# Results of the last two expert positions summed in idle PSUM banks by matmul; second layer's bias rows loaded as start values of its sums

## What is computed

```
sel_group = jnp.argmax(grp_score, axis=-1)                 # one of 4 groups
_, idx = lax.top_k(jnp.where(in_group, biased, -jnp.inf), TOP_K)   # two experts in it
wts = sel_aff / jnp.sum(sel_aff, axis=-1, keepdims=True)
for e in range(N_EXPERTS):
    he = jax.nn.silu(h @ w_gate[e]) * (h @ w_up[e])
    y = y + combine[..., e:e + 1] * (he @ w_down[e])
x_l = x_l + mod_l[5] * y_l
```

## Time and profile before

| | |
|---|---|
| median of 3 executions | 1031.48 us (1030.33 to 1037.86) |
| the profiled execution | 1036.62 us, its span 1034.8 us |
| mean granted TensorE clock | 0.853 of full speed |
| PE busy | 781.3 us (76%), 6820 instructions |
| DVE busy | 392.3 us (38%), 883 instructions |
| ACT busy | 178.6 us (17%) |
| POOL busy | 28.0 us (3%) |
| DMA | 320.53 MB, mean 310 GB/s |
| SP's queue | 282.88 MB, 69.9% of 16 engines' span |

### The profile page before, as it was taken

The page is one execution under the profiler, slowest core; times in us unless marked ns, Lnnn a source line. Parts: engine busy times, 40 slices in busy tenths (PEclk is TensorE's granted clock), DMA queues, the critical chain, the costliest instruction groups (busy, mean ns, idle before and its releaser), DMA issues.

```text
span 1034.8 us, 18303 instructions
## 1 busy us (share of the span) xinstructions
PE 781.3 (76%) x6820; PEld 433.2 (42%) x6821; DVE 392.3 (38%) x883; ACT 178.6 (17%) x381; POOL 28.0 (3%) x43
## 2 busy tenths in 40 slices
PE   3989899997959549976669953596478878798580
PEld 1534647544544225543235521272344444354240
DVE  2267879647978642120112101623512111121013
ACT  3211011115530201110111100420111111111001
POOL 0000000020000010000000001000000000000001
PEclk9899999799989669996779976799599898799785
DMA  9887988789507788589999899902789899999923
GB/s 346 297 300 254 343 296 286 274 303 320 213 1 269 302 342 346 215 350 415 418 417 414 337 416 396 404 20 102 294 307 365 325 416 417 414 417 415 415 82 127
DMA packets 102222, 320.53 MB, mean 310 GB/s; under 512 B 12315, under 2 KB 27547, under 8 KB 85667
## 3 DMA queue, kind: packets, MB, share of 16 engines
q1 hardware_dynamic: 78454, 282.88, 69.9%
q0 software_dynamic: 3952, 21.37, 5.4%
q10 hardware_dynamic: 19776, 15.75, 4.7%
HBM read 303.58 MB, written 24.64 MB: 317 GB/s over the span
## 4 chain that ended last, share of the span: by engine, by line
PE 30%; issue 27%; DVE 14%; DMA 13%; SPq 11%; ACT 1%; POOL 1%; ACTq 1%; DVEq 0%; POOLq 0%
PE bank L1469 7%; SPq L492 6%; DMA raw<-in_w_up 5%; DMA arena<-unit_rows 5%; PE bank L1678 3%; PE bank L1602 3%; PE bank L1785 3%; PE bank L1473 2%; DVE arena L873 2%; DMA arena<-in_ada_b 2%; PE bank L1691 2%; PE bank L1459 1%; PE bank L1478 1%; SPq L457 1%; DMA bias<-in_ada_b 1%
## 5 line engine op out<-in xcount | busy, mean ns | idle before, releaser
L1678 PE MATMUL bank<-raw,arena 128*32 128x256 f32 x3392 | 251.6, 441 | 73.2 <-DMA raw<-in_w_up 41.5
L1678 PEld LDWEIGHTS bank<-raw,arena 128*32 128x32 f32 x3392 | 120.5, 124 | 184.0 <-DMA raw<-in_w_up 57.1
L1285 DVE TENSOR_TENSOR arena<-arena,bank 64x256 f32<-64x256 f32 x53 | 22.5, 425 | 345.8 <-ACT arena L784 345.8
L1691 PE MATMUL bank<-raw,arena 128*32 128x256 f32 x1696 | 112.7, 393 | 0.8 <-DVE arena L1273 0.8
L1691 PEld LDWEIGHTS bank<-raw,arena 128*32 128x32 f32 x1696 | 60.8, 115 | 40.3 <-issue 5.6
L1469 PE MATMUL bank<-ring,arena 128*128 128x512 f32 x160 | 72.3, 611 | 0.0
L873 DVE SCALAR_TENSOR_TENSOR bias<-ring,small,bias 128x512 f32<-128x512 f32 x84 | 63.2, 752 | 3.0
L1665 PE MATMUL bank<-consts_sb,arena 64*128 64x64 f32 x212 | 37.0, 298 | 33.8 <-DVE arena L1285 17.2
L784 ACT ACTIVATE arena<-bank 64x256 f32<-64x256 f32 x53 | 19.9, 376 | 237.8 <-PE bank L1678 219.2
L1665 PEld LDWEIGHTS bank<-consts_sb,arena 64*128 64x128 f32 x212 | 29.4, 198 | 43.9 <-issue 23.6
L1469 PEld LDWEIGHTS bank<-ring,arena 128*128 128x128 f32 x160 | 31.2, 196 | 39.0 <-issue 39.0
(11 more groups left out here) (229 smaller groups left out, 792.5 us busy)
## 6 DMA issues: line engine op xcount, KB each, us to landing
raw<-in_w_gate SPq DMA_DIRECT2D x64, 1024.0 KB, 18.5
raw<-in_w_up SPq DMA_DIRECT2D x64, 1024.0 KB, 20.6
raw<-in_w_down SPq DMA_DIRECT2D x64, 1024.0 KB, 22.0
ring<-in_ada_w SPq DMA_DIRECT2D x24, 2048.0 KB, 13.3
ring<-in_w_in SPq DMA_DIRECT2D x7, 2048.0 KB, 10.9
unit_results<-arena ACTq DMA_DIRECT2D x244, 32.0 KB, 7.1
arena<-unit_rows ACTq DMA_DIRECT2D x55, 128.0 KB, 6.9
ring<-in_w_out SPq DMA_DIRECT2D x2, 2048.0 KB, 32.8
```

The source lines that it names most:

```text
L1678: ins = mm(ps[4][o:o + S, 0:FW], xT[:, i, j * S:(j + 1) * S], w[:, k % 4, h * FW:(h + 1) * FW], start=(k == 0), stop=(k == KD - 1))
L1691: ins = mm(ps[5][j * S:(j + 1) * S, 0:XW], hT_e[:, k % QN, k // QN * S:(k // QN + 1) * S], w[:, k % 2, j * XW:(j + 1) * XW], start=(k == 0 ...
```

## The change

Five things change.

1. Layer 1's `ada_b` rows are loaded in SP's stream like those of layer 0, into partition 0 of a second pair of buffers `bias1` (it lies where the Fourier table `dft` comes later), and are the start value of the chunk's sum. The three row loads and the three `add_bias1` are gone; the first of the eight DVE instructions of chunks 12 to 23 now adds too. The table `dft` is loaded after layer 0's experts.
2. The results of the units of the last two expert positions (14 and 15, `LATE = 14`) are not stored. `late_tables` and `late_rows` prepare per layer, in 128x512 tables, each token's place and share; for each late unit `scatter_weights` makes a 32x128 matrix of shares per token tile, and `scatter` on PE multiplies it with the unit's result into banks 0 to 3, eight matmuls with 32 rows each, accumulating.
3. `all_stored` comes before the late units, so POOL's four fetches run beside them, with `share_early`, which is zero for late results.
4. `combine_results` does its four weighted additions and then adds the four banks in eight instructions.
5. SP loads the `ada_sums` and `dft` directly behind the last expert's weights and `fnet` after the fetches; ACT copies only eight of the twelve sums ahead of `norm2`.

```diff
-                if n and STREAM[n - 1][0] == "ada" and 4 <= STREAM[n - 1][1] < N_ADA:
+                if n and STREAM[n - 1][0] == "ada" and STREAM[n - 1][1] >= 4:
                     load_bias(STREAM[n - 1][1])
...
-            sp.wait_ge(L[0]["expert_closed"], NE - 2)
+            sp.wait_ge(L[0]["expert_closed"], NE - 1)
+            for p in range(3):
+                sp.dma_start(mods[:, AT1[2 * p]:AT1[2 * p] + 2, :].rearrange("p a (b n) -> p (a b) n", b=2),
+                             scratch[4 * p:4 * p + 4].rearrange("c p n -> p c n")).then_inc(acc_back[p], 16)
+            sp.dma_start(K_[:, K_PARTS[2]:K_PARTS[3]], consts[:, K_PARTS[2]:K_PARTS[3]]).then_inc(dft_in, 16)
+            for t in range(TT):
+                sp.wait_ge(y_back[t], 32)
             for hf in range(2):
                 sp.dma_start(slot(FNET_AT + hf), fnet_v[:, :, hf * W:(hf + 1) * W]).then_inc(fnet_in[hf], 16)
...
+            sp.wait_ge(added, TT)
             load_experts(1, fnet_used)
...
-                n = act.snap(units, min_val=NE, max_val=MAX_UNITS)
-                store_y(n, n * S, 0)
-                act.wait_ge(E["x_landed"], n * 16 + 16)
-                for place in range(2):
-                    act.wait_ge(E[f"y_stored{place}"], (NE // 2 + 1) * 16 * JN)
+                n_tok = act.value_load(cnt_i[0:1, LATE:LATE + 1], min_val=0, max_val=SEQ)
+                n = act.snap(units, min_val=0, max_val=MAX_UNITS)
+                unit(n)
+                act.wait_ge(E["y_stored1"], (LATE // 2 + 1) * 16 * JN)
...
+                nc.scalar.copy(s_done[:, l:l + 1], ident[:, 0:1]).then_inc(all_stored, 1)
+                store_y(n, n * S, 0)
+                act.reg_add(units, units, 1)
+                late_units(n_tok)
...
+            def late_tables(l):
+
+                for b in range(2):
+                    dve.wait_ge(acc_saved[b], 16 * (N_ADA // 2))
+                for b, cols in enumerate((rel, share)):
+                    for t in range(TT):
+                        for q in range(2):
+                            at = (2 * t + q) * P
+                            ins = nc.vector.tensor_scalar(bias[:, b, at:at + P], ident, cols[:, t, q:q + 1], None,
+                                                          ALU.mult)
+                ins.then_inc(p_ready, 1)
...
+                def scatter_weights(done):
+
+                    nc.vector.scalar_tensor_tensor(late_T.rearrange("p t q n -> p (t q n)"), rel_row, late_at,
+                                                   share_row, ALU.is_equal, ALU.mult).then_inc(E["late_ready"], 1)
+                    dve.wait_ge(E["late_ready"], done + 1)
+                    nc.vector.tensor_tensor(late_T[:, :, 0, :], late_T[:, :, 0, :], late_T[:, :, 1, :], ALU.add
+                                            ).then_inc(E["late_ready"], 1)
...
+                def late_unit():
+
+                    n = dve.snap(units, min_val=1, max_val=MAX_UNITS)
+                    turn_back(n - 1)
+                    product(n)
+                    late_result(n - 1)
+                    turned(n + 1)
+                    m = dve.snap(late, min_val=1, max_val=MAX_UNITS)
+                    dve.wait_ge(E["scattered"], m)
+                    nc.vector.tensor_scalar(late_at, late_at, float(S), None, ALU.add).then_inc(E["late_ready"], 1)
+                    dve.wait_ge(E["late_ready"], m * 3)
+                    scatter_weights(m * 3)
...
+                dve.wait_ge(L[l]["scattered"], late)
+                for t in range(TT):
+                    for j in range(JN):
+                        part = xl[:, t, j * XW:(j + 1) * XW]
+                        ins = nc.vector.tensor_tensor(part, part, ps[j][:, t * XW:(t + 1) * XW], ALU.add)
                     ins.then_inc(added, 1)
...
+                pe.wait_ge(p_ready, 2 * l + 2)
+                mm(ps[2][:], ones, bias[:, 0, :], start=True, stop=True)
+                mm(ps[3][:], ones, bias[:, 1, :], start=True, stop=True).then_inc(rank_ps, 1)
                 further(pe.value_load(cnt_i[0:1, 0:1], min_val=0, max_val=SEQ), own)
...
+                def scatter(n):
+
+                    m = pe.snap(late, min_val=1, max_val=MAX_UNITS)
+                    pe.wait_ge(E["y_ready"], n + 1)
+                    pe.wait_ge(E["late_ready"], m * 3 - 1)
+                    for t in range(TT):
+                        for j in range(JN):
+                            ins = mm(ps[j][:, t * XW:(t + 1) * XW],
+                                     late_T[j * S:(j + 1) * S, t, 0, :], ys[j * S:(j + 1) * S, 1, :], start=False,
+                                     stop=False, skip_group_check=True)
+                    ins.then_inc(E["scattered"], 1)
+                    pe.reg_add(late, late, 1)
...
+                def late_unit(prev, own, begins):
+
+                    n = pe.snap(units, min_val=1, max_val=MAX_UNITS)
+                    next_unit(prev, own, begins)
+                    scatter(n)
```

More of the change, by code:

```diff
@@ L61 @@
                   ("lt", P), ("gt", P), ("mask", 3 * P), ("iota", 2 * S), ("ones", P), ("first4", NG),
-                  ("first16", NE), ("steps", UN), ("dft", TT * 2 * SEQ)):
+                  ("first16", NE), ("steps", UN), ("lane", 1), ("dft", TT * 2 * SEQ)):
     CONSTS[_name] = (_at, _at + _n)
@@ L125 @@
 HELD = 3
+LATE = NE - 2
 RAWS = HELD * NH
@@ L263, in program @@
                       for n in ("ys", "Pg", "Ph"))
-        y_of = (f_, lay([("second", (TT, D))], 2 * D)[0]["second"])
+        y_of = ([f_[:, t, :] for t in range(TT)], [bias[:].rearrange("p a n -> p (a n)"), arena[:, 3 * D:4 * D]])
         fT = lay([("fT", (KD, SEQ))], KD * W + 4 * D)[0]["fT"]
@@ L778, in experts, with unit @@
                     store_y(0, LISTED + (place - 1) * S, place)
-                def next_unit(place):
-                    n = act.snap(units, min_val=0, max_val=MAX_UNITS)
+                def unit(n):
                     act.wait_ge(E["gate_up_done"], n + 1)
@@ L789, in next_unit, with late_units @@
                     load_x(n + 3)
+                def next_unit(place):
+                    n = act.snap(units, min_val=0, max_val=MAX_UNITS)
+                    unit(n)
                     store_y(n, n * S, place)
                     act.reg_add(units, units, 1)
+                def late_units(n_tok):
+                    with act.If(n_tok > S):
+                        with act.Fori(1, UN) as u:
+                            with act.If(n_tok > u * S):
+                                unit(act.snap(units, min_val=0, max_val=MAX_UNITS))
+                                act.reg_add(units, units, 1)
                 act.wait_ge(rows_out, 16 * 2 * TT * (l + 1))
@@ new lines, in late_further @@
+                def late_further(n_tok):
+                    with dve.If(n_tok > S):
+                        with dve.Fori(1, UN) as u:
+                            with dve.If(n_tok > u * S):
+                                late_unit()
+                n_tok = dve.value_load(cnt_i[0:1, LATE:LATE + 1], min_val=0, max_val=SEQ)
+                next_unit(0, LATE // 2)
+                for b in range(4):
+                    nc.vector.memset(ps[b][:], 0.0)
+                scatter_weights(0)
+                dve.wait_ge(E["y_stored1"], (LATE // 2 + 1) * 16 * JN)
@@ L1359, in _ @@
             route(0)
-            experts(0)
-            for p in range(3):
-                add_bias1(p)
-            combine_results(0)
+            combine_results(0, experts(0))
             norm_mod(3, 5, mod1[1], mod1[0], (gain_late, 16), 8 + 2)
```

142 lines of the change are left out of this document (90 added, 52 removed).

## The result

On record the changed kernel took 1055.26 us (median of five) beside 1036.07 for before: 1.0181 times as long, interval 1.0135 to 1.0226. So it is slower by 14 to 19 us, where 0.5 us was forecast (1032.0), and outside the range (to 1043). The forecast of 1032.0 stands on a median of 1031.48 for before, which is 4.6 us of the distance to 1055.26 and no more. Single executions of 1196 to 3298 us, of before, of the changed kernel (one of its five on record: without it the median is 1053.8) and of some others, are left out of every ratio. The trace shown here is that of `after_again`, span 1048.2 us for 1034.8 of before: 13.4 us more.

What follows compares the result with a forecast made beforehand. It took full DMA engines to bound the expert stages, with time winnable only at the seams. 12.6 + 4.0 - 17.3 + 4.0 - 2.8 = +0.5 us on the profiled 1036.62, 1032.0 from the median 1031.48; range 1021 to 1043.

Steps and rivals of the forecast that it cites:

- The output projection, a loss: Output projection: `w_out` queued behind a waiting bias row lands at about 325.5, PE starts 10.5 us late; +12.6 us.
- The end of layer 0, -17.3 us: End of layer 0's experts: the norm step L933 starts at 646.3 instead of 663.65; bounds -14 and -20.
- 3.2 MB at 399 GB/s is 8 us, so it lands at 634.6: End of layer 0: landing of the first `ada_sums` load, sharing the DMA with 2.1 MB of fetches.
- four additions at once: End of layer 0: DVE does the four weighted additions straight after the last result, 5.2 us, till 637.7.
- The tables, +4.0 in each stage: Start of each expert stage: eight multiplies and two 512-column matmuls delay turn_he; +4.0 us per layer, bounds 3.0 and 6.0.
- The scatter, 0.9 us: Late units: eight 32-row matmuls run four at a time, 0.9 us, plus 0.4 wait; +1.3 us per scatter between units.
- one at a time: Rival on the scatter: row tiles run serially, 3.4 us per scatter, total 1042.4 us; chance 0.12.
- The end of layer 1, -2.8: End of layer 1: scatters +3.9, shorter tail after the last result -7.9, fetches +1.2; bounds -6 and +1.
- The fetches take the last experts' DMA time fully: Rival, both layers' ends: 2.1 MB of fetches cost 5.3 us in each layer; +7, 1039 us; chance 0.12.
- The unrolled bodies stall PE: Rival: three expert bodies per layer are new code whose stalls show in layer 1; +5 to +8, about 1038; chance 0.09.

Runs made afterwards that it cites:

- after_again: The changed kernel unaltered, measured again on another chip beside before: 1048.65 us, 1.0154 times before.
- e_fetch_late: Changed kernel, `w_out` ahead of last two bias rows, tables behind expert position 13, layer 0's fetches held until the second sums load landed: 1026.54 us, 0.9936 of before.
- e_no_fetch: Changed kernel with `w_out` ahead of the last two bias rows and layer 0's four fetches replaced by plain 16-column loads: 1020.52 us, 0.987 of before.
- nine kernels with the matmul part: The changed kernel and its variants that keep scatter and late units, against before: from 1020.52 us to 1055.26 us.
- fold kernels: Before with only bias rows folded into the sums and `dft` loaded late: 1045.01 us; with the last two rows behind `w_out`, 1031.03 and, repeated, 1031.63 us.

## Why the prediction was wrong, point by point

*The output projection, a loss: right.* PE started at 327.78, which is 2.3 us behind the 325.5 of the text, 1.3 of it because the attention ended later. The block itself took 15.63 us for 14.00, 1.6 lost to the clock for the 2.1 of the text. So the loss is 14.4 us at unit 0; it reads as +12.7 at unit 1 because PE did unit 0's gate and up in 3.66 us, for 5.31 before, and then waits for ACT all the same. Undoing the order alone took back 12.2 us of the time. The mechanism, the order in SP's queue, is shown.

*The end of layer 0, -17.3 us: the step that failed, by 7.5 us.* The mechanism was right in part (results earlier, no bias rows). The last result was forecast at 632.5 and is 633.5 with the shift of 19.7 taken off. The failing term is "3.2 MB at 399 GB/s is 8 us, so it lands at 634.6". It released PE 13.4 us after its issue, at 641.3 with the shift off, 6.7 us behind that place: 5.4 in the transfer, 1.3 in the later issue. In the window from 648 to 661 the engines moved 345 GB/s, so 4.5 MB: of these SP's queue had 2.29 MB, of which the first sum is 1.05, and POOL's fetches 2.04. So some 1.2 MB of SP's other loads, the end of the last weights and the two sums issued right behind the first, shared the engines with it. The 3.2 MB left them out (3.3 us at 399 GB/s), and the rate was lower (2.1 us). In `e_fetch_late` and `e_no_fetch`, with no fetch in its way, PE could take it 6.8 us after the issue, so the fetches, issued 2 us ahead of the sums, hold them back by at least 6.6 us, more than the 5.3 us of all their bytes at 400 GB/s. The "four additions at once" failed too, which by itself cost nothing: the fetches went out at 625.9 (shift off) for 622, and `xl` is complete at 646.3 for 641.0, but ACT is not free before 651.7. I had also timed the seam as a chain of waits and gave it a transfer time only at one link, when the earlier trace rows showed a full DMA in it: in the seam's table the order of the bytes is nearly free and their number counts. From the first sum to L952 it took 13.9 us for 11.7: PE had been idle and came back at a granted clock of 0.50, so its first sums took twice their time. Together the norm step is 9.0 us behind its forecast (655.3 for 646.3); some 1.4 of them came back by unit 28, in the Fourier layer, which I did not look into.

*The tables, +4.0 in each stage: size right, stage wrong.* Each piece came as costed: eight multiplies 1.66 us (1.6), the two matmuls 775.32 to 778.68, 3.4 us (3.3). But the stages lost 7.1 and 6.4 us. What the rest is, ACT's first silu of each stage shows, which both kernels wait for; before and then changed:
```profile
388.27 0.38 ACT L784 ACTIVATE arena<-bank 64x256 f32<-64x256 f32 x1
760.70 0.38 ACT L784 ACTIVATE arena<-bank 64x256 f32<-64x256 f32 x1
```
```profile
403.27 0.38 ACT L782 ACTIVATE arena<-bank 64x256 f32<-64x256 f32 x1
772.29 0.38 ACT L782 ACTIVATE arena<-bank 64x256 f32<-64x256 f32 x1
```
It is shifted by 15.0 and 11.6 us, where PE's transposes just ahead of it, the borders of my table, are shifted by 12.7 and 9.9. From it to the next transpose (units 2 and 29, +19.1 and +15.5) the tables cost 4.1 and 3.9 us, as forecast. The 2.3 and 1.7 us ahead of it are not theirs. In layer 0 they are mostly PE's faster first gate and up, a loss of the output projection that the border hid. In layer 1 they are ACT's: its first load of a unit's rows waits for POOL's four writes of them, and goes out 8.1 us after the last write's issue for 6.6 before. That is 7.9 to 8.2 us in each of the nine kernels with the matmul part, tables moved or not, and 6.8 to 7.7 in the fold kernels; why, no run tells. Behind units 2 and 29 come 0.6 us, and 0.9 net of the stall.

*The scatter, 0.9 us: right.* 1.15 us for eight matmuls, where one at a time would have been 3.4; that rival is out. The Trainium skill, TensorEngine Tiling (Array Packing), Tiling Modes, lets 32-row tiles run four at a time; the trace agrees with it, and the 0.25 us above my sum is all that a drain between modes could have cost. Between the last units a scatter and the wait ahead of it made each unit 1.36 us longer (from turn to turn 7.67 us, 1005.50 to 1013.17, for 6.31, 988.20 to 994.51), for 1.3 forecast.

*The end of layer 1, -2.8: near.* The units up to 54 cost 3.6 us for 5.1, the tail brought 6.6 for 7.9: 3.0 us together.

*The rivals.* "The fetches take the last experts' DMA time fully" was the one to believe for layer 0; I gave it +7 us in all and 12 in 100; at that seam alone the fetches are worth 7.3 us, where my sum held about half of their 5.3. "The unrolled bodies stall PE": one stall is new, 2.7 to 4.0 us at a place that I had not named, and it nets 0.9 us in its stage; the loop's exit shows 3.11 us for 2.72 before. That before has four such stalls inside layer 1's loop I had overlooked. The sum of the terms that missed (7.5, 3.1, 2.4, 0.1, less 1.5 and plus 1.3) is 12.9 us, which is the distance from +0.5 to +13.4.

The range failed as well: each bound was taken for one term, and the two largest misses, the seam and the stages, went the same way.

## What to carry to other kernels

Where a window shows the DMA engines full across a seam, forecast the seam from its bytes first and from its chain of waits second, and count in them whatever is issued right behind the load that is waited for: in this seam bringing one transfer forward sent another one back (2 us either way), and only fewer bytes (7.3 us) or less work behind the last of them (2.6 us) gained. A one-row load placed in the queue ahead of a large one hands the large one its own wait; ask for each load in a shared queue what stands behind it. Set-up work of a few us belongs where its engines wait for weights, not at a stage's start, where two engines hand work to each other and all of it shows. And put the borders of a table of shifts at the instruction that the next stage waits for: PE's own start times moved by up to 1.7 us with its clock alone.

## What was not expected of the hardware

- Entering the first expert of the loop in layer 1, PE shows 2.7 to 4.0 us of "issue" in the kernels with three more expert bodies; before and the kernels with the fold alone have none at that unit. Stalls of 2.5 to 4.6 us stand at units 33, 35, 41 and 47 of before and, but for one, of every other kernel with 55 units. Whether it is the length of the program or its place was not tried.
- While four fetches and three loads of the sums were under way, from 648 to 661 us, the engines moved 345 GB/s at a busy share of 0.96, against 398 to 415 in the expert stages; over the whole seam it was 379.
- Eight 32-row matmuls of 256 columns into four banks took 1.15 us, the same in every kernel at full clock, and 2.09 us at the lower.
